# A fused decoder step: five staging buffers, three more at the turn, two DMA streams moved to ScalarE, and another order at the exchanges

## The reference

```
up = rmsnorm(x, g_ffn) @ w_up                        # 1024 -> 2 x 2816
upc, ffn_buf_new = causal_conv(ffn_buf, up, ffn_conv_w)   # width 3
u, gt = split(upc)
x = x + (silu(gt) * u) @ w_down                      # 2816 -> 1024
y = rmsnorm(x, g_final)
```

## Time and profile before

| | |
|---|---|
| median of 3 runs | 1099.85 us (1098.59 to 1101.6) |
| the profiled execution | 1101.41 us, of which the span is 1099.7 us |
| PE busy | 1049.0 us, 95% of the span |
| DVE busy | 876.5 us, 80% |
| ACT busy | 535.2 us, 49% |
| POOL busy | 44.7 us, 4% |

### The profile page before, as it was taken

The page is one execution under the profiler, slowest core; times in us unless marked ns, Lnnn a source line. Parts: engine busy times, 40 slices in busy tenths (PEclk is TensorE's granted clock), DMA queues, the critical chain, the costliest instruction groups (busy, mean ns, idle before and its releaser), DMA issues.

```text
span 1099.7 us, 17773 instructions
## 1 busy us (share of the span) xinstructions
PE 1049.0 (95%) x6610; PEld 1016.3 (92%) x6610; DVE 876.5 (80%) x1522; ACT 535.2 (49%) x960; POOL 44.7 (4%) x162
## 2 busy tenths in 40 slices
PE   7999999999999999999999999999997699988996
PEld 7999988888999999999999999999997599988995
DVE  6953788898899988878878878888865787977956
ACT  7444444666444644444544544544543444455743
POOL 0100000000000000000000000000000000000022
PEclk9999999999999999999999999999999799989998
DMA  7311201115434122222222222222267826365243
GB/s 255 97 37 44 96 25 35 39 59 193 118 122 147 39 77 97 97 77 97 97 77 98 96 77 97 97 77 97 89 192 249 291 68 208 105 205 160 90 136 130
DMA packets 68101, 123.40 MB, mean 112 GB/s; under 512 B 5520, under 2 KB 51344, under 8 KB 67984
## 3 DMA queue, kind: packets, MB, share of 16 engines
q1 hardware_dynamic: 64608, 117.89, 32.1%
q10 hardware_dynamic: 3408, 4.38, 1.1%
HBM read 95.76 MB, written 27.53 MB: 112 GB/s over the span
## 4 chain that ended last, share of the span: by engine, by line
PE 53%; DVE 10%; DMA 5%; issue 3%; ACT 2%; SPq 0%; DVEq 0%; ACTq 0%
PE psum L2579 38%; PE psum L2635 10%; DMA zb<-act_d 4%; PE psum L2555 2%; PE psum L2610 2%; DVE att L2047 1%; DVE h_lo L2052 1%; DVE x_sb L1812 1%; DVE zb L1469 1%; DMA raw<-in_w 0%; DVE x_sb L2071 0%; DVE x_sb L2064 0%; DVE hx_lo L2052 0%; DVE att L1805 0%; PE psum L2640 0%
## 5 line engine op out<-in xcount | busy, mean ns | idle before, releaser
L2579 PE MATMUL psum<-h_hi,act_hi 128*128 128x344 f32 x336 | 107.6, 320 | 0.0
L2579 PE MATMUL psum<-h_hi,act_lo 128*128 128x344 f32 x336 | 107.6, 320 | 0.0
L2579 PE MATMUL psum<-h_lo,act_hi 128*128 128x344 f32 x336 | 107.6, 320 | 0.0
L2579 PE MATMUL psum<-h_hi,w_lo 128*128 128x344 f32 x336 | 107.4, 320 | 0.0
L2579 PE MATMUL psum<-h_hi,w_hi 128*128 128x344 f32 x336 | 107.3, 319 | 0.0
L2579 PE MATMUL psum<-h_lo,w_hi 128*128 128x344 f32 x336 | 107.1, 319 | 0.0
L2579 PEld LDWEIGHTS psum<-h_hi,act_hi 128*128 128x128 f32 x336 | 63.5, 189 | 0.0
L2579 PEld LDWEIGHTS psum<-h_hi,act_lo 128*128 128x128 f32 x336 | 63.4, 189 | 0.0
L2579 PEld LDWEIGHTS psum<-h_lo,act_hi 128*128 128x128 f32 x336 | 63.4, 189 | 0.0
L2579 PEld LDWEIGHTS psum<-h_hi,w_hi 128*128 128x128 f32 x336 | 63.1, 188 | 0.1
L2579 PEld LDWEIGHTS psum<-h_hi,w_lo 128*128 128x128 f32 x336 | 63.2, 188 | 0.0
(11 more groups left out here) (367 smaller groups left out, 3395.2 us busy)
## 6 DMA issues: line engine op xcount, KB each, us to landing
raw<-in_w SPq DMA_DIRECT2D x76, 512.0 KB, 3.8
zb<-act_d SPq DMA_DIRECT2D x45, 344.0 KB, 4.3
act_d<-x_sb SPq DMA_DIRECT2D x11, 1032.0 KB, 5.4
raw<-in_w SPq DMA_DIRECT2D x24, 384.0 KB, 3.5
att<-in_w SPq DMA_DIRECT2D x15, 512.0 KB, 4.6
act_d<-att SPq DMA_DIRECT2D x11, 516.0 KB, 2.7
x_sb<-in_x SPq DMA_DIRECT2D x8, 516.0 KB, 5.0
x_d<-x_sb ACTq DMA_DIRECT2D x12, 344.0 KB, 2.5
```

The source lines that it names most:

```text
L2579: ins = mm(bank[to], a, b, start=(fresh and k == p == 0), stop=(k == HALF - 1 and p == 2), skip_group_check=True)
```

## The change

1. Staging: five buffers in rotation in place of three (`rstd`, the three in `s_flat`, `pad_u`), and three more (the parts of `pair_buf`) for items 0, 1 and 2. `stage_of`, `stage_before` and `stage_uses` say which item uses which; each buffer has its own semaphore and its own first condition in `load_item`.
2. SP's order: items 0 to 3 are loaded as soon as pair 9 is stored, before the last two weight loads of the up-projection's loop; then the other items, with counts per load changed at the exchanges.
3. The store of the last pair and the five loads of the residual leave SP and are issued by ACT (`store_last_pair`, `load_x2`), between its `t_hi`s.
4. ACT's and DVE's order at the turn: items 4 to 11 and the T splits change places, items 16 and 17 are split after `preload(0)` on ACT, `unit_sums(0)` stands before `t_lo(3, 1)` and waits for the last pair's store, and the reads of T0 and T1 stand elsewhere. `tap_2(21, 1)` stands before `t_lo(1, 1)`.
5. `item_hi` of group 0 waits for the product that last read the place it writes, not for the last product of unit 21.
6. The load of the square root's table moves from ahead of `s_hi(0, "a22")` to the unit S6's splits in group 1.
7. At the exchanges DVE does the `s_read`s of the last unit ahead of the item halves and of the second `t_lo`.

```diff
+EARLY = 3
+STAGES = 5
+SKIP_U = 52
+def stage_of(n):
+    if n < EARLY:
+        return STAGES + n
+    return 1 if n == SKIP_U else (n - EARLY) % STAGES
...
-        stage = [s_flat[:, o:o + 2 * TW].rearrange("p (c t) -> p c t", c=2) for o in (0, 2 * TW, 4 * TW)]
+        stage = [b.rearrange("p (c t) -> p c t", c=2) for b in (
+            rstd[:, 0:2 * TW], s_flat[:, 0:2 * TW], s_flat[:, 2 * TW:4 * TW], s_flat[:, 4 * TW:6 * TW], pad_u[:, 0:2 * TW],
+            pair_buf[:, 0:2 * TW], pair_buf[:, 2 * TW:4 * TW], pair_buf[:, 4 * TW:6 * TW])]
...
-                if n < 3:
+                before = stage_before(n)
+                if before is not None:
+                    sp.wait_ge(act_split, before + 1)
+                elif n < EARLY:
+                    sp.wait_ge(act_stored, 32 * (NG - 1))
+                elif n == EARLY + STAGES - 1:
+                    sp.wait_ge(conv_done, 2 * (NF - 1) + 1)
+                    sp.wait_ge(state_out, 2 * NF)
+                elif n > EARLY:
                     sp.wait_ge(part_lo_ready, parts_by(NF - 1))
                 else:
-                    sp.wait_ge(act_split, n - 2)
+                    sp.wait_ge(x_ready, len(X_PARTS))
...
+                if n == NF:
+                    for k in range(4):
+                        load_item(k)
-            for q in (4, 5, 6):
+            for q in range(4, 8):
                 load_down(q)
-            load_item(4)
...
-            store_pair(NG - 1)
...
-            sp.dma_start(x_sb[:, :, tile(2)], x2_d[:, :, tile(2)]).then_inc(x2_last_back, 16)
...
+            for q in range(8, 12):
+                load_item(2 * q - 8)
+                load_item(2 * q - 7)
+                load_down(q)
...
-                more = {("S", 0): (1, 1), ("S", 1): (1, 1), ("S", 2): (1, 1), ("S", 3): (3, 4), ("T", 4): (2, 2), ("T", 5): (1, 0),
-                        ("S", 6): (1, 2), ("S", 7): (3, 3), ("T", 6): (2, 2), ("T", 7): (1, 0),
+                more = {("S", 0): (1, 1), ("S", 1): (1, 1), ("S", 2): (2, 2), ("S", 3): (2, 4), ("T", 4): (2, 2),
+                        ("S", 6): (2, 3), ("S", 7): (1, 4), ("T", 6): (2, 2),
...
             t_hi(1, 1)
+            item_hi(4)
+            item_hi(5)
             silu(NF - 1)
             t_hi(2, 0)
-            item_hi(4)
-            item_hi(5)
-            t_hi(2, 1)
             item_hi(6)
             item_hi(7)
+            t_hi(2, 1)
+            store_last_pair()
+            for n in range(8, 12):
+                item_hi(n)
             t_hi(3, 0)
-            item_hi(8)
-            item_hi(9)
+            load_x2()
             t_hi(3, 1)
-            item_hi(10)
-            item_hi(11)
+            item_hi(12)
+            item_hi(13)
...
                     preload(u)
+                    if u == 0:
+                        item_hi(16)
+                        item_hi(17)
...
# DVE, last unit of a group that another follows:
-                        else:
-                            item = X_N[g + 1, "b11", 0] - 1
-                            item_lo(item)
-                            item_lo(item + 1)
                         s_read(u, "p5")
                         t_lo(T_PAIRS[g + 1][0], 0)
                         s_read(u, "p6")
                         if not fin:
+                            item = X_N[g + 1, "b11", 0] - 1
+                            item_lo(item)
+                            item_lo(item + 1)
+                        s_read(u, "p2")
+                        if not fin:
                             item_lo(item + 2)
                             item_lo(item + 3)
-                        s_read(u, "p2")
-                        if not fin:
-                            item_lo(item + 4)
-                            item_lo(item + 5)
+                        s_read(u, "p7")
                         t_lo(T_PAIRS[g + 1][0], 1)
-                        s_read(u, "p7")
```

More of the change, by code:

```diff
@@ L290, with stage_before, stage_uses @@
 X_N = numbered(X_ITEMS)
+EARLY = 3
[5 more added lines that the diff above has]
+    return 1 if n == SKIP_U else (n - EARLY) % STAGES
+def stage_before(n):
+    return max((k for k in range(n) if stage_of(k) == stage_of(n)), default=None)
+def stage_uses(n):
+    return sum(stage_of(k) == stage_of(n) for k in range(n + 1))
 def halves_of(split):
@@ L664, in item_stage @@
             ks = item_chunks(item)
-            return stage[(X_N[item] - 1) % 3][:, 0:ks.stop - ks.start, :]
+            return stage[stage_of(X_N[item] - 1)][:, 0:ks.stop - ks.start, :]
         def item_home(homes, item):
@@ L725, in load_item @@
                 j, (row, t) = GROUP_PAIR0[g], X_ROW[name]
-                if n < 3:
+                before = stage_before(n)
[7 more added lines that the diff above has]
+                elif n > EARLY:
                     sp.wait_ge(part_lo_ready, parts_by(NF - 1))
                 else:
-                    sp.wait_ge(act_split, n - 2)
+                    sp.wait_ge(x_ready, len(X_PARTS))
                 sp.wait_ge(act_stored, 32 * (j + GROUP_PAIRS[g]))
[L731 to L736, removed]
+                sp.dma_start(item_stage(item), act_d[j + ks.start:j + ks.stop, row, :, tile(t)].rearrange("k p t -> p k t")).then_inc(act_landed[stage_of(n)], 16)
             for p in range(4):
@@ L1382, in _ @@
                     s_hi(u + 1, "S4")
+                    if u == S_UNITS[1][1]:
+                        nc.scalar.activation(small[:, 62:63], eps[:, 0:1], ACT.Sqrt)
                     if fin:
@@ L2163, in _ @@
             tap_1(NF - 1, 1)
+            tap_2(NF - 1, 1)
             t_lo(1, 1)
-            tap_2(NF - 1, 1)
             tap_1(NF - 1, 0)
             tap_2(NF - 1, 0)
+            item_lo(4)
+            item_lo(5)
             act_mult(NF - 1)
@@ L2170, in _ @@
             t_lo(2, 0)
-            item_lo(4)
-            item_lo(5)
-            t_lo(2, 1)
             item_lo(6)
             item_lo(7)
+            t_lo(2, 1)
+            for n in range(8, 12):
+                item_lo(n)
             t_lo(3, 0)
-            item_lo(8)
-            item_lo(9)
+            unit_sums(0)
             t_lo(3, 1)
-            unit_sums(0)
-            item_lo(10)
-            item_lo(11)
+            item_lo(12)
+            item_lo(13)
+            s_lo(0, "a11")
+            s_lo(0, "S1")
             for i in range(2):
                 t_read(0, i)
[L2185 to L2189, removed]
             s_lo(0, "S2")
             s_lo(0, "a12")
+            t_read(1, 0)
             t_read(1, 1)
-            t_read(2, 0)
             item_lo(14)
@@ L2197, in _ @@
             s_lo(0, "S4")
-            t_read(2, 1)
-            for i in range(2):
-                t_read(3, i)
+            for tp in (2, 3):
+                for i in range(2):
+                    t_read(tp, i)
             for g in range(3):
@@ L2237, in _ @@
                         else:
-                            item_lo(item + 6)
-                            item_lo(item + 7)
+                            item_lo(item + 4)
+                            item_lo(item + 5)
                         s_read(u, "p3")
@@ L2242, in _ @@
                             mid_add(u, "p7")
+                        else:
+                            item_lo(item + 6)
+                            item_lo(item + 7)
                         continue
```

43 lines of the change are left out of this document (20 added, 23 removed).

## The result

The changed kernel takes 1091.24 us in the median of 4 runs (1090.19 to 1092.73), against 1099.62 for the kernel before on the same chip: ratio 0.9923 with a 95% interval from 0.9904 to 0.9942. It is 8.4 us faster. The prediction said 18.4 faster, 1081. The profiled execution took 1092.73 us, its span 1090.8.

A forecast was written before the change was run, and what follows sets the result against it. PE was taken as the bound, its waits and slow clock from 800 us on as the gain's ceiling (40.0 us). 10.3 + 2.8 + 5.3 = 18.4 us off the profiled 1101.4 gave 1083.0, median 1081; range 1071 to 1091.

The forecast's parts named there:

- Part 1: Start of the turn: items 0 to 3 go out earlier, so the `read_v3` wait and its slow clock go: 3.9 us.
- Part 2: T pairs at the turn: T3 starts 2 us late, its second half in time, where two waits cost 8.3: 6.3 us go.
- Part 3: Unit S0 at the turn: `preload` wait goes, p7 starts at 865.3 against 876.99; 10.3 us for the turn (bounds 3.3, 13.7).
- Part 4: First exchange: the wait at p4 of S3 goes, p7 of S4 stays 1.3 late; gain 2.8 us (bounds 0, 3.8).
- Part 5: Second exchange: p4 of S7 only 1.0 late, p1 of S8 waits 4.6; gain 5.3 us (bounds 0, 11.9).
- rival A: At the exchanges DVE's order only passes the wait on, its work being the same: gain there 0, 1089.5 us; chance 0.08.

The follow-up runs named there:

- h7: f5 with items 0 to 3 issued behind the last two weight loads of the up-projection's loop, as before the change: 1080.57 us, ratio 0.9820.
- f5: e2 with the four residual loads of tiles t0 and t1 moved from ScalarE to SP, behind item 17: 1077.03 us, ratio 0.9797.
- f4: e2 with the four residual loads of tiles t0 and t1 cut to 8 columns each, still issued on ScalarE: 1078.54 us, ratio 0.9814.
- e2: The changed kernel with DVE's old order at the exchanges (item halves and second `t_lo` ahead of the reads): 1081.88 us, ratio 0.9838.
- f12: The kernel before with only the new order of DVE's bank reads at the exchanges, three buffers: 1110.74 us, ratio 1.0109.
- e3: The changed kernel with DVE's old order and SP's old counts per load at the exchanges, five buffers kept: 1082.49 us, ratio 0.9844.
- h1: f5 with T3's first split ahead of items 10 and 11, and S0's p5 and p6 reads ahead of items 16, 17 and `unit_sums(1)`: 1077.70 us.
- f8: The changed kernel with DVE's old read order and three staging buffers in rotation instead of five: 1101.25 us, ratio 1.0017.

## Why the prediction was wrong

**Part 1 held.** Items 0 to 3 were issued at 801.14 and item 0's high part ran at 804.24, 3.1 us later (3.0 taken). `read_v3` no longer held PE. h7 gives the price at its place, 4.2 for 3.9; of that, 2.5 to 3.5 us reached the total there.

**Part 2 held in sum.** T3 started 2.6 us late (2 forecast), `item_hi(10)` ran at 836.36 (landing forecast near 836). The issues were mis-sized: the four loads took 3.85 us, 0.96 each, where the earlier trace rows had 0.37; ACT stood idle for 3.0 of it. (My 2.5 for the five was no sum either: four at 0.37 and one at 0.6 are 2.1.) T3's second half had its operands in time even so. T3's wait was followed by 1.5 us of slow clock, which I had not counted.

**Part 3 held, with the wait at two places.** p7 of S0 started at 866.91, 865.3 forecast; item 17 was in at 859.7, 859 forecast. I had no wait left at p6, and there were 4.7 us of it: items 14 and 15, on which `preload` stands, came as late as the residual made them, which I had reckoned for items 16 and 17 alone. p7's wait was smaller by as much, 3.2 where 8 to 10 was forecast. The turn gave 9.6 against 10.3, so the agreement is partly luck: two waits that I had not foreseen, or had too small, stood against one that I had too large. The residual's first load I had landing at 847.5 from a sum that gives 846.5 (1.41 MB at 0.165 MB/us are 8.5 us, not 9.5); it took 9.5, and p1 of S0 did not wait.

From the rule of the Trainium skill ("DMA: Bandwidth & Descriptors", Issuing engines are not separate DMA queues) I had worked out 7.9 for the turn; the 9.6 measured lies nearer to my 10.3. Two runs agree with the rule in kind: f5, with the same four loads on SP behind the items, is 4.9 us faster, and f4, which still issues them on ScalarE but nearly without bytes, gains about as much (their intervals overlap). Issuing those four on ScalarE saved nothing that can be seen.

**Part 4 failed**, at the sentence "Now that read comes ahead of them, and its halves 24 and 25 have a buffer free early: the wait goes." The wait at p4 of S3 went, and p7 of S4 waits 1.5 (1.3 forecast). But I had counted DVE's work up to p7 of S4 as the same and passed over p1 of S4, which now waits 2.6 for a `t_read`. Gain -0.4 in place of 2.8.

**Part 5 failed in the same step.** p4 of S7 waits 0.9 (1.0 forecast). From the read of p7 to p1 of S8 I counted 17.3 us of DVE's work, with 1.6 for `t_hi(6, 1)`; it took 990.75 - 968.63 = 22.1. The 1.6 was there (1.69); what was missing is the 4.14 us for which DVE stood ahead of `unit_sums(8)`. The chain from an `item_lo` over the staging buffer and SP's order to the next weights was in the prediction only as the argument for rival A ("buffers come free later"), and had no price. I had set against it that the reads come earlier in every case. They do, by 0.9 us. The two gains were also rounded up without a row: 3.8 - 1.3 is 2.5 and not 2.8, and the 4.9 became 5.3.

So the step that failed is the same in both parts: the new order of DVE's reads was taken as cheap (0.8 us lost at p1 of S8, nothing at p1 of S4), because only DVE's own work was counted behind it. The runs show it as the one thing measured in the change that costs time, 9.7 us with five buffers (e2) and 11 with three (f12). Against that stands a gain that I had too small: with five buffers and the old reads the exchanges lose some 10 us less than before (e3), more than the 8.1 that I gave to buffers and reads together. e2's 1082 lies at the predicted 1081, but not for my reasons. Rival A's time (1089.5) was near the result, and its mechanism, a wait passed on at no cost, is refuted by f12 and e2.

The best kernel measured is f5, at 0.9797 [0.9782, 0.9811], and h1 equals it: the change without its seventh part, and with the residual behind the items, is 14 us faster than the change itself. Left open is how the 5.4 us at the second exchange of f5 could go.

## What to carry to other kernels

When an instruction is moved behind one that waits for the bottleneck, price what it frees (a buffer, then the queue that stands at that buffer, then everything that this queue issues afterwards), not only its own engine's work. A DMA that is wanted late belongs behind those wanted early, whichever engine issues it (4.9 us here). Of a change in several parts, put each part back alone before the sum is believed: here two parts of 10 us with opposite signs looked like one of nothing.

## What was not expected of the hardware

A DMA issue on ScalarE took 0.366 us in the first half, where the DMA engines moved 124 GB/s, and 0.96 us at 838 us in the changed kernel, where four followed each other directly while the items were being read. What makes the difference is open. It is not the bytes of the load: f4's four, of 8 KB each, took 3.71 us together. Nor is it shown to be the traffic: in the kernel before SP issued the same four loads between 849.9 and 863.9 us at 0.46 us each, one of them at 858.4 us with the DMA engines 93% busy at 323 GB/s; in f5 SP issued them directly after each other in 2.66 us.

From 836 to 856 us the DMA engines of the changed kernel moved 376 GB/s, more than the 320 of the earlier trace rows. The rate that I had taken for the ceiling of the transfers was not one. In f8 the same window showed 329 GB/s.

The slow clock followed waits unevenly. At the turn waits of 2.56, 4.73 and 3.17 us were each followed, at once or within 2 us, by 10 to 12 matmuls that started 0.29 us apart, and the granted clock of these stretches was 0.50 to 0.55; behind the wait of 2.60 us at 927.84 in the same kernel they started 0.16 apart from the second on, at a granted clock of 1.00. The length of the wait alone does not decide it.
